# One core, a state-space block and a recurrent/attention block: the passage between them, where x1 is turned and made h

## The chip, the cores and the metric

The kernel runs on one core of a Trainium2 chip (trn2). The metric is the device time of one launch in microseconds. All inputs and outputs are float32.

## The reference, cut to what matters

Two blocks follow each other on x, 512 positions of 2048 columns. Both are computed in full; here is what stands around the passage between them.

```python
def first_block(x, ln_g, final_g, ...):
    x = x + ssm_mixer(rmsnorm(x, ln_g[0]), ...)     # ends with y @ ssm_w_out
    return rmsnorm(x, final_g)

def second_block(x, c, positions, w_ada, b_ada, w_in, ...):
    mod = silu(c) @ w_ada[l] + b_ada[l]
    shift, scale, gate = jnp.split(mod, 3, axis=-1)
    h = rms_norm(x) * (1.0 + scale[:, None, :]) + shift[:, None, :]
    proj = h @ w_in[l]                              # 2048 x 4160, float32
    ...                                             # recurrent branch, attention branch
    x = x + gate[:, None, :] * (y @ w_out[l])
```

## The kernel before, in words

**Matmuls.** Each float32 operand of a large product is split in two rounded parts, hi and lo, and a product is three matmuls of 128 x 128 x 512 into one bank of the accumulator memory (hi by hi, hi by lo, lo by hi). `three` (L2401) issues them; `three_hi_first` (L2406) issues the two that need only the hi part of the moving operand, then waits for its lo part and issues the third. It is used where the moving operand is only just being made.

**Weights** come in units. A unit of the second block's input projection holds 4 blocks of 128 rows by 256 columns, so two column blocks n = 0 and 1 of 128. Four units (16 blocks of rows) make a panel. Units go through a ring of 4 places: SP starts the load into `w_raw` (L669), ScalarE writes `w_hi` (L1090), VectorE writes `w_lo` (L1771). TensorE signals `unit_used` after a unit's last matmul.

**The passage.** The first block's projection out ends with its last panel. VectorE adds the residual, ScalarE sums squares, and meanwhile TensorE runs 36 turns of the identity (`keep_running(36)`, L2586). Then VectorE has the factor `x1rr` of each position (L1898), and x1, which lies with positions on the partitions, must become h with model columns on the partitions. A block of h is 128 model columns by 512 positions; there are 16 of them, kb = 0 to 15. The steps of one block:

- scaling: `xh <- x1t * x1rr`, in pieces of 512 columns (four blocks) by 128 positions. For the first 512 columns VectorE does positions t = 0 and 1 (`scale_x1`, L1902 to L1910) and ScalarE t = 2 and 3 (L1198). For the other columns VectorE does all four, partly between its other work (L1911 to L1921);
- turn: TensorE transposes the block, four 128 x 128 pieces (`turn_x1`, L2588, the transposes at L2596), into one of banks 4 to 7. The signal is `h_turned`;
- ScalarE writes `h_mod`, with the shift and scale (`modulate`, L1202 to L1207), and `h_hi` (`make_h_hi`, L1209 to L1211);
- VectorE writes `h_lo = h_mod - h_hi` (L1923).

ScalarE's order is written out by hand (L1213 to L1222): modulate(0), make_h_hi(0), modulate(1), and then for kb = 1 to 15 modulate(kb+1) and make_h_hi(kb), with the split of unit 2's weights behind kb = 3 and that of unit 3's behind kb = 7. VectorE's loop (L1913 to L1926) does for each kb the scaling that falls due and then `h_lo`; behind kb = 4 and 8 it makes `w_lo` of units 2 and 3. Units 0 and 1 have been split before. Each of these loops runs in order on its engine, and each instruction waits on semaphores that count blocks.

**TensorE's order** in the first panel (L2620 to L2623): blocks 0 to 3 are turned, then units 0 to 3 follow (`first_panel`, L2600). In a unit, column block n = 0 goes first: three matmuls with each of its 4 blocks of h, and behind each block of h the turn of the block four further on. Then n = 1 follows with 12 matmuls on blocks of h that are there already. Results of n = 0 gather in bank 0, those of n = 1 in bank 1. After the panel ScalarE copies the two banks to `xr` (L1232), and the other panels run on with all of h in place (`panels`, L2626).

Of the kernel before, what the change touches and what calls it, by code (L numbers as in the profile page):

```python
# [17 lines left out]
ACT = mybir.ActivationFunctionType  # L18
AX_X = mybir.AxisListType.X

P = 128
SEQ = 512
NT = SEQ // P
D = 2048
KB = D // P
# [18 lines left out]
UKT = 4  # L44
UCOL = 256
UNIT = UKT * UCOL
UPP = KB // UKT
# [29 lines left out]
TKT, TCOL = 2, 512  # L77
# [4 lines left out]
OUT_PANELS = D // TCOL  # L82
# [3 lines left out]
U_RNN = U_OUT1 + OUT_PANELS * OUT1_UPP  # L86
# [31 lines left out]
ADA_PARTS = P // ADA_ROWS  # L118
ADA_FETCH_AT, ADA_FOLD_AT = (1, 9), (5, 13)
ADA_COL = (0, 48, 128, 176, 256)  # L120
LAST_X1 = (OUT_PANELS - 1) * TCOL


# [68 lines left out]
def build_program(nc, x, ln_g, final_g, ssm_w_in, ssm_conv_w, ssm_conv_b, ssm_dt_bias, ssm_a_log, ssm_d,  # L192
# [4 lines left out]
    with ctx:  # L197
        sem_names = {}

        def sem(name):  # L200
            assert name not in sem_names
            sem_names[name] = ctx.enter_context(nc.semaphore(name))
            return sem_names[name]

        def sb(name, shape, dt=F32, scope=ctx):
            return scope.enter_context(nc.sbuf_tensor(name, shape, dt))
# [8 lines left out]
        ps = ctx.enter_context(nc.psum_tensor("ps", [P, 8, 512], F32))  # L215
# [3 lines left out]
        w_hi = sb("w_hi", [P, RING, UNIT], F32R)  # L219
        w_lo = sb("w_lo", [P, RING, UNIT], F32R)  # L220
# [9 lines left out]
        x1gs, x1rr = small[:, 56:60], small[:, 60:64]  # L230
# [88 lines left out]
        def ada_cols(k):  # L319

            return cols[:, ADA_COL[k]:ADA_COL[k] + ADA_FOLD]

# [14 lines left out]
        h_hi = sb("h_hi", [P, KB, SEQ], F32R, scope_f)  # L337
        h_lo = sb("h_lo", [P, KB, SEQ], F32R, scope_f)
# [57 lines left out]
        x1t = sb("x1t", [P, NT, D], F32, scope_e)  # L396
        xh = sb("xh", [P, NT, D], F32, scope_e)
# [32 lines left out]
        lo_ready = sem("lo_ready")  # L430
        unit_used = sem("unit_used")
# [70 lines left out]
        xh_ready = sem("xh_ready")  # L502
        h_turned = sem("h_turned")
        h_mod_ready = sem("h_mod_ready")
        h_hi_ready = sem("h_hi_ready")
        h_lo_ready = sem("h_lo_ready")
# [3 lines left out]
        f_bank_freed = sem("f_bank_freed")  # L510
# [59 lines left out]
        def unit_ap(ring, slot, cols_=UCOL):  # L570
            return ring[:, slot, 0:UKT * cols_].rearrange("p (k n) -> p k n", k=UKT)
# [351 lines left out]
        def _(act):  # L923
# [32 lines left out]
            for kb in range(KB):  # L956
                if kb % UKT == 0:
                    hi(0, kb // UKT)
                if kb == 3 * UKT:
# [5 lines left out]
                                     scale=cols[:, ROW_LN + kb:ROW_LN + kb + 1]).then_inc(hn_hi_ready, 1)  # L965
# [172 lines left out]
            def x1_last_squares():  # L1138

                i = OUT_PANELS - 1  # L1140
                for t in range(NT):
                    act.wait_ge(x1_added, i * NT + t + 1)
                    act.wait_ge(x1_squared, i * NT + t)
                    if t == 0:
# [4 lines left out]
                    act.wait_ge(x1g_squared, i * NT + t)  # L1149
                    nc.scalar.activation(ps[:, 5, :], xh[:, t, LAST_X1:], ACT.Square, accum_out=x1_part[:, 1, t:t + 1]  # L1150
                                         ).then_inc(x1g_squared, 1)
                act.dma_start(x1_tok[:, :, LAST_X1:], xh[:, :, LAST_X1:]).then_inc(x1_free, 16)

# [24 lines left out]
            for i in range(1, OUT_PANELS):  # L1178
                last = i == OUT_PANELS - 1
# [15 lines left out]
                nc.scalar.activation(r, r, ACT.Sqrt).then_inc(root_done, 1)  # L1195
            act.wait_ge(x1_rms_ready, 1)
            for t in (2, 3):
                nc.scalar.activation(xh[:, t, 0:TCOL], x1t[:, t, 0:TCOL], ACT.Copy, scale=x1rr[:, t:t + 1]  # L1198
                                     ).then_inc(xh_half_ready, 1)
            act.wait_ge(ada_cols_ready, 1)  # L1200

# [14 lines left out]
            for kb in range(1, KB):  # L1216
# [3 lines left out]
                if kb in (3, 7):  # L1220
                    u = (kb + 1) // UKT + 1
                    split_hi(U_RNN + u, u, landed_before(U_RNN) + 1)  # L1222
            act.wait_ge(h_turned, KB)
            act.wait_ge(xh_ready, NT * OUT_PANELS - 2)
            for u in range(UPP):
                if u == UPP - 1:
                    for n in range(2):
# [235 lines left out]
        def _(dve):  # L1463
# [345 lines left out]
            def x1_panel(i):  # L1809
                dve.wait_ge(x_in_landed, i * 16 + 16)  # L1810
                for t in range(NT):
# [8 lines left out]
                    if i == OUT_PANELS - 1:  # L1820
                        if t == 0:
                            dve.wait_ge(unit_used, U_RNN - OUT1_UPP // 2)
                        nc.vector.tensor_tensor(xh[:, t, LAST_X1:], x1p[:, t, :], gateb[:, LAST_X1:], ALU.mult
                                                ).then_inc(x1g_ready, 1)
# [74 lines left out]
            dve.sem_inc(f_bank_freed, 2)  # L1899
            dve.wait_ge(x1_rms_ready, 1)  # L1900

            def scale_x1(c, t):  # L1902
                at = slice(c * TCOL, (c + 1) * TCOL)
                if c == OUT_PANELS - 1 and t == 0:
                    dve.wait_ge(x1_free, 16 * (OUT_PANELS + 1))
                src = x1t[:, t, at] if c < OUT_PANELS - 1 else xh[:, t, at]
                nc.vector.tensor_scalar(xh[:, t, at], src, x1rr[:, t:t + 1], None, ALU.mult).then_inc(xh_ready, 1)

            for t in range(2):
                scale_x1(0, t)  # L1910
            for t in range(2):  # L1911
                scale_x1(1, t)
            for kb in range(KB):  # L1913
                if kb == 4:
                    dve.wait_ge(root_done, NT + 3)
                    st.done(nc.vector.reciprocal(x1rs, x1rs))
                if kb == 1:
                    for t in range(2, NT):
                        scale_x1(1, t)
                if 1 <= kb <= KB - 8:  # L1920
                    scale_x1((kb - 1) // 4 + 2, (kb - 1) % 4)  # L1921
                dve.wait_ge(h_hi_ready, kb + 1)
                nc.vector.tensor_tensor(h_lo[:, kb, :], h_mod[:, kb % 4, :], h_hi[:, kb, :].bitcast(F32),  # L1923
                                        ALU.subtract).then_inc(h_lo_ready, 1)
                if kb in (UKT, 2 * UKT):
                    split_lo(U_RNN + kb // UKT + 1, kb // UKT + 1)  # L1926
# [430 lines left out]
        def _(pe):  # L2357
# [43 lines left out]
            def three(out_, a_hi, a_lo, b_hi, b_lo, start, stop):  # L2401
                nc.tensor.matmul(out_, a_hi, b_hi, start=start, stop=False)  # L2402
                nc.tensor.matmul(out_, a_hi, b_lo, start=False, stop=False)  # L2403
                return nc.tensor.matmul(out_, a_lo, b_hi, start=False, stop=stop)  # L2404

            def three_hi_first(out_, w_hi_, w_lo_, a_hi, a_lo, start, stop, hi_sem, lo_sem, count):  # L2406

                pe.wait_ge(hi_sem, count)
                nc.tensor.matmul(out_, w_hi_, a_hi, start=start, stop=False)  # L2409
                nc.tensor.matmul(out_, w_lo_, a_hi, start=False, stop=False)  # L2410
                pe.wait_ge(lo_sem, count)
                return nc.tensor.matmul(out_, w_hi_, a_lo, start=False, stop=stop)  # L2412
# [156 lines left out]
            for u in range(len(LAST_SCAN), OUT1_UPP):  # L2569
                if u == Y_HALF // TKT + 3:  # L2570

                    pe.wait_ge(y_squared, 2)
                    for t in range(NT):
                        mm = nc.tensor.matmul(ps[:, 4, t:t + 1], ysq[:, t * P:(t + 1) * P], ones[:, 0:1],
                                              start=True, stop=True)
# [11 lines left out]

            def turn_x1(kb):  # L2588

                pe.wait_ge(xh_ready, kb // 4 * NT + 2)  # L2590
                if kb == 0:
                    pe.wait_ge(xh_half_ready, 2)
                if kb >= 4:
                    pe.wait_ge(h_lo_ready, kb - 3)
                for t in range(NT):
                    mm = nc.tensor.transpose(ps[:, 4 + kb % 4, t * P:(t + 1) * P], xh[:, t, kb * P:(kb + 1) * P],  # L2596
                                             ident[:])
                mm.then_inc(h_turned, 1)

            def first_panel(u):  # L2600

                pe.wait_ge(lo_ready, U_RNN + u + 1)
                for n in range(2):
                    if u == 0:
                        pe.wait_ge(f_bank_freed, n + 1)
                    for k in range(UKT):
                        kb = u * UKT + k
                        w = [unit_ap(r, u)[:, k, n * P:(n + 1) * P] for r in (w_hi, w_lo)]
                        if n == 0:
                            mm = three_hi_first(ps[:, n, :], *w, h_hi[:, kb, :], h_lo[:, kb, :],  # L2610
                                                kb == 0, kb == KB - 1, h_hi_ready, h_lo_ready, kb + 1)
                        else:
                            mm = three(ps[:, n, :], *w, h_hi[:, kb, :], h_lo[:, kb, :], kb == 0, kb == KB - 1)
                        if n == 0 and kb + UKT < KB:
                            turn_x1(kb + UKT)
                    if n == 0 and u == UPP - 1:
                        mm.then_inc(f_bank_done, 1)
                mm.then_inc(unit_used, 1)

            for kb in range(UKT):  # L2620
                turn_x1(kb)
            for u in range(UPP):
                first_panel(u)  # L2623
            pe.wait_ge(h_lo_ready, KB)

# [29 lines left out]
            for u in range(KR_UNITS):  # L2655
                pe.wait_ge(lo_ready, U_KR + u + 1)
                for k in range(UKT):
                    kb = u * UKT + k
                    w = unit_ap(w_hi, u, 2 * ROPE)[:, k, :]
                    if kb == 0:  # L2660
                        nc.tensor.matmul(ps[:, 2, :], w, h_hi[:, kb, :], start=True, stop=False)
                    mm = nc.tensor.matmul(ps[0:ROPE, 2, :], w[:, 0:ROPE], h_lo[:, kb, :], start=False, stop=False)
                    if kb:
                        mm = nc.tensor.matmul(ps[:, 2, :], w, h_hi[:, kb, :], start=False, stop=kb == KB - 1)
# [262 lines left out]
```

## Time and profile before

| | |
|---|---|
| median of 3 runs | 2118.04 us (2118.0 to 2118.15) |
| the profiled execution's own time | 2117.97 us |
| its span, first to last instruction | 2116.4 us |
| TensorE matmul busy | 2103.2 us, 99% of the span |
| VectorE busy | 1302.8 us, 62% |
| ScalarE busy | 806.0 us, 38% |
| DMA | 139 GB/s over the span |

Engines are named PE (TensorE matmul), PEld (its weight loads, which overlap the matmuls), DVE (VectorE), ACT (ScalarE), POOL (GpSimd) and SP. Times in the trace are microseconds from the span's start. A matmul of 512 columns is shown with 0.40 us, but the next starts 0.233 us later: their ends overlap, so the step from start to start is what one costs. The same holds for the vector engines, whose next instruction often starts before the last is shown ended. L12 is line 12 of the kernel; transposes of the passage are "MATMUL ps<-ident,xh" at L2596, those of `three_hi_first` are at L2409, L2410 and L2412.

### The profile page before, as it was taken

The numbers are of one execution on the slowest core, as the hardware profiler recorded it, in microseconds if no ns is written. First come the engines' busy times: TensorE is split into PE (matmuls) and PEld (weight loads), VectorE is DVE, ScalarE is ACT, GpSimd is POOL, SyncE is SP. The second block draws the span as 40 slices with busy tenths as digits, with TensorE's granted clock in tenths as the row PEclk, the third lists the DMA queues.
The fourth block names the chain that finished last, engine by engine and source line by source line (L and its number), as shares of the span: only waits on it lengthen the run. The fifth ranks groups of instructions, "written<-read, shape, count | busy, mean of one in ns | idle before, by whom it ended". The sixth has DMA issues, their size and how long they took to land.

```text
span 2116.4 us, 27861 instructions
## 1 busy us (share of the span) xinstructions
PE 2103.2 (99%) x10059; PEld 1683.0 (80%) x10059; DVE 1302.8 (62%) x2147; ACT 806.0 (38%) x1089; POOL 88.0 (4%) x130
## 2 busy tenths in 40 slices
PE   8999999999999999999999999999999999999999
PEld 7888888888888888888878888878887778876887
DVE  5567867777786777778874323253227788667333
ACT  5233433333343342434443222262224556665121
POOL 0000000000000000000000000000000001110000
PEclk9999999999999999999999999999999999999999
DMA  7555645555564555555564354343333232112332
GB/s 221 166 156 152 184 149 167 162 168 163 159 175 147 171 158 165 162 170 170 187 218 155 111 162 133 107 144 108 99 89 84 78 104 79 63 60 74 126 119 99
DMA packets 234242, 294.50 MB, mean 139 GB/s; under 512 B 36883, under 2 KB 170883, under 8 KB 233411
## 3 DMA queue, kind: packets, MB, share of 16 engines
q1 hardware_dynamic: 200402, 252.98, 38.6%
q0 software_dynamic: 8624, 29.04, 4.9%
q10 hardware_dynamic: 25152, 11.64, 2.1%
q8 instruction: 39, 0.64, 0.1%
q14 instruction: 25, 0.20, 0.0%
HBM read 273.54 MB, written 20.08 MB: 139 GB/s over the span
## 4 chain that ended last, share of the span: by engine, by line
PE 95%; DVE 3%; DMA 1%; ACT 1%; issue 0%; SPq 0%; DVEq 0%; ACTq 0%
PE ps L2402 29%; PE ps L2404 29%; PE ps L2403 29%; PE ps L2503 2%; PE ps L2485 1%; PE ps L2736 1%; PE ps L2761 1%; DMA xt<-in_x_dram 1%; PE ps L2740 1%; PE ps L2752 0%; PE ps L2648 0%; PE ps L2487 0%; PE ps L2412 0%; PE ps L2409 0%; PE ps L2410 0%
## 5 line engine op out<-in xcount | busy, mean ns | idle before, releaser
L2402 PE MATMUL ps<-hn_hi,w_hi 128*128 128x512 f32 x1264 | 500.9, 396 | 0.0
L2404 PE MATMUL ps<-hn_hi,w_lo 128*128 128x512 f32 x1264 | 499.3, 395 | 0.0
L2403 PE MATMUL ps<-hn_lo,w_hi 128*128 128x512 f32 x1264 | 499.2, 395 | 0.0
L1771 DVE TENSOR_TENSOR w_lo<-w_raw,w_hi 128x1024 fp32r<-128x1024 f32 x174 | 212.8, 1226 | 399.6 <-ACT w_hi L1090 398.3
L1090 ACT ACTIVATE w_hi<-w_raw 128x1024 fp32r<-128x1024 f32 x174 | 183.2, 1057 | 450.2 <-PE ps L2404 412.1
L953 ACT ACTIVATE w_hi<-w_raw 128x1024 fp32r<-128x1024 f32 x162 | 170.9, 1056 | 413.1 <-PE ps L2404 396.4
L1509 DVE TENSOR_TENSOR w_lo<-w_raw,w_hi 128x1024 fp32r<-128x1024 f32 x162 | 198.1, 1223 | 205.6 <-ACT w_hi L953 205.5
L2402 PEld LDWEIGHTS ps<-hn_hi,w_hi 128*128 128x128 f32 x1264 | 237.0, 187 | 58.4 <-issue 1.2
L2404 PEld LDWEIGHTS ps<-hn_hi,w_lo 128*128 128x128 f32 x1264 | 236.9, 187 | 57.9
L2403 PEld LDWEIGHTS ps<-hn_lo,w_hi 128*128 128x128 f32 x1264 | 237.0, 187 | 57.2
L2402 PE MATMUL ps<-w_hi,y_hi 128*128 128x512 f32 x512 | 203.0, 396 | 0.4 <-DVE y_lo L1780 0.4
L2404 PE MATMUL ps<-w_hi,y_lo 128*128 128x512 f32 x512 | 202.5, 395 | 0.0
L2403 PE MATMUL ps<-w_lo,y_hi 128*128 128x512 f32 x512 | 202.5, 395 | 0.0
L2402 PE MATMUL ps<-h_hi,w_hi 128*128 128x512 f32 x496 | 197.1, 397 | 0.0
L2403 PE MATMUL ps<-h_lo,w_hi 128*128 128x512 f32 x496 | 195.9, 395 | 0.0
L2404 PE MATMUL ps<-h_hi,w_lo 128*128 128x512 f32 x496 | 195.9, 395 | 0.0
L1606 DVE SCALAR_TENSOR_TENSOR ada_acc<-ada_raw,silu_c,ada_acc 128x768 f32<-128x768 f32 x120 | 121.4, 1012 | 0.3 <-DMA ada_raw<-in_w_ada_dram 0.3
L2402 PEld LDWEIGHTS ps<-h_hi,w_hi 128*128 128x128 f32 x496 | 93.0, 187 | 28.8 <-issue 6.5
L2402 PEld LDWEIGHTS ps<-w_hi,y_hi 128*128 128x128 f32 x512 | 96.2, 188 | 24.6 <-DVE y_lo L1780 1.3
L2404 PEld LDWEIGHTS ps<-w_hi,y_lo 128*128 128x128 f32 x512 | 96.2, 188 | 23.3
L2403 PEld LDWEIGHTS ps<-w_lo,y_hi 128*128 128x128 f32 x512 | 96.2, 188 | 22.9
L2404 PEld LDWEIGHTS ps<-h_hi,w_lo 128*128 128x128 f32 x496 | 93.0, 187 | 22.6
(392 smaller groups left out, 2765.0 us busy)
## 6 DMA issues: line engine op xcount, KB each, us to landing
ada_raw<-in_w_ada_dram SPq DMA_DIRECT2D x128, 384.0 KB, 3.4
w_raw<-in_ssm_w_in_dram SPq DMA_DIRECT2D x96, 512.0 KB, 4.6
w_raw<-in_ssm_w_in_dram SPq DMA_DIRECT2D x128, 256.0 KB, 4.0
w_raw<-in_w_in_dram SPq DMA_DIRECT2D x64, 512.0 KB, 3.8
w_raw<-in_ssm_w_out_dram SPq DMA_DIRECT2D x60, 512.0 KB, 3.5
csb<-cs_rows POOLq DMA_DIRECT2D x32, 512.0 KB, 7.2
w_raw<-in_w_out_dram SPq DMA_DIRECT2D x32, 512.0 KB, 4.0
y_rows<-yt POOLq DMA_DIRECT2D x8, 1024.0 KB, 4.7
```

Source lines behind the costliest of these rows:

```text
L953: nc.scalar.activation(w_hi[:, s, :], w_raw[:, s, :], ACT.Copy).then_inc(hi_ready, 1)
L1090: nc.scalar.activation(w_hi[:, slot, :], w_raw[:, slot, :], ACT.Copy).then_inc(hi_ready, 1)
L1509: nc.vector.tensor_tensor(w_lo[:, s, :], w_raw[:, s, :], w_hi[:, s, :].bitcast(F32), ALU.subtract).then_inc(lo_ready, 1)
L1606: ins = nc.vector.scalar_tensor_tensor(ada_acc[:], ada_raw[:, k % 2, :], silu_c[:, k:k + 1], ada_acc[:], ALU.mult, ALU.add)
L1771: nc.vector.tensor_tensor(w_lo[:, slot, :], w_raw[:, slot, :], w_hi[:, slot, :].bitcast(F32), ALU.subtract).then_inc(lo_ready, 1)
L2402: nc.tensor.matmul(out_, a_hi, b_hi, start=start, stop=False)
L2403: nc.tensor.matmul(out_, a_hi, b_lo, start=False, stop=False)
L2404: return nc.tensor.matmul(out_, a_lo, b_hi, start=False, stop=stop)
L2485: nc.tensor.transpose(ps[:, 4, b * P:(b + 1) * P], xst[:, b, at], ident[:])
L2503: mm = nc.tensor.matmul(ps[h * HD:(h + 1) * HD, 6, b * P:(b + 1) * P], lhs[:, 2 * b + h, :], rhs[:, 2 * b + h, :], start=first, stop=c == ...
L2736: nc.tensor.matmul(ps[:, bank, 0:n], qt[:, h, at], kt[:, h, 0:n], start=True, stop=False)
L2740: nc.tensor.matmul(ps[:, bank, 0:n], qpt[rows, at], kpt[rows, 0:n], start=False, stop=True).then_inc(scored, 1)
```

## The change

Three things, all in the passage. The first 128 columns are scaled alone: ScalarE scales only those for t = 2 and 3, VectorE those for t = 0 and 1 and then, in four instructions, the remaining 384 of the first 512 columns for all four t. Unit 0 is a function of its own, `first_unit`: each of its 4 blocks of h is multiplied with both column blocks (four matmuls on h_hi, two on h_lo), and the next turn follows. And only three blocks are turned ahead, in place of four, in all units of the panel. The counts of the waits follow.

```diff
@@ -118,6 +118,7 @@
+H_AHEAD = 3
@@ -1195,7 +1196,7 @@
             for t in (2, 3):
-                nc.scalar.activation(xh[:, t, 0:TCOL], x1t[:, t, 0:TCOL], ACT.Copy, scale=x1rr[:, t:t + 1]
+                nc.scalar.activation(xh[:, t, 0:P], x1t[:, t, 0:P], ACT.Copy, scale=x1rr[:, t:t + 1]
                                      ).then_inc(xh_half_ready, 1)
@@ -1221,7 +1222,7 @@
-            act.wait_ge(xh_ready, NT * OUT_PANELS - 2)
+            act.wait_ge(xh_ready, NT * OUT_PANELS + 2)
@@ -1899,15 +1900,17 @@
-            def scale_x1(c, t):
-                at = slice(c * TCOL, (c + 1) * TCOL)
+            def scale_x1(c, t, first=0, last=TCOL):
+                at = slice(c * TCOL + first, c * TCOL + last)
...
             for t in range(2):
-                scale_x1(0, t)
+                scale_x1(0, t, last=P)
+            for t in range(NT):
+                scale_x1(0, t, first=P)
             for t in range(2):
                 scale_x1(1, t)
@@ -2587,7 +2590,7 @@
             def turn_x1(kb):
 
-                pe.wait_ge(xh_ready, kb // 4 * NT + 2)
+                pe.wait_ge(xh_ready, kb // 4 * NT + NT + 2 if kb else 2)
                 if kb == 0:
                     pe.wait_ge(xh_half_ready, 2)
@@ -2601,8 +2604,6 @@
                 for n in range(2):
-                    if u == 0:
-                        pe.wait_ge(f_bank_freed, n + 1)
                     for k in range(UKT):
...
-                        if n == 0 and kb + UKT < KB:
-                            turn_x1(kb + UKT)
+                        if n == 0 and kb + H_AHEAD < KB:
+                            turn_x1(kb + H_AHEAD)
...
-            for kb in range(UKT):
+            def first_unit():
+
+                pe.wait_ge(lo_ready, U_RNN + 1)
+                pe.wait_ge(f_bank_freed, 2)
+                for kb in range(UKT):
+                    w = [[unit_ap(r, 0)[:, kb, n * P:(n + 1) * P] for r in (w_hi, w_lo)] for n in range(2)]
+                    pe.wait_ge(h_hi_ready, kb + 1)
+                    for n in range(2):
+                        nc.tensor.matmul(ps[:, n, :], w[n][0], h_hi[:, kb, :], start=kb == 0, stop=False)
+                        nc.tensor.matmul(ps[:, n, :], w[n][1], h_hi[:, kb, :], start=False, stop=False)
+                    pe.wait_ge(h_lo_ready, kb + 1)
+                    for n in range(2):
+                        mm = nc.tensor.matmul(ps[:, n, :], w[n][0], h_lo[:, kb, :], start=False, stop=False)
+                    if kb == UKT - 1:
+                        mm.then_inc(unit_used, 1)
+                    turn_x1(kb + H_AHEAD)
+
+            for kb in range(H_AHEAD):
                 turn_x1(kb)
-            for u in range(UPP):
+            first_unit()
+            for u in range(1, UPP):
                 first_panel(u)
             pe.wait_ge(h_lo_ready, KB)
```

## Rows read from the trace of the kernel before

**Rows 1.** The page, busy time, share of the span and instructions of each engine.

```profile
PE 2103.2 (99%) x10059; PEld 1683.0 (80%) x10059; DVE 1302.8 (62%) x2147; ACT 806.0 (38%) x1089; POOL 88.0 (4%) x130
```

**Rows 2.** Waits of PE, whole run: total us, times, longest.

```profile
PE ps L2596 <- ACT xh L1198: 1.2, 1, 1.2
```

**Rows 3.** Timeline of PE, 1391 to 1408: start, us, instruction, [idle before <-releaser].

```profile
1391.16 4.09 PE L2581 MATMUL ps<-ident 128*128 128x128 f32 x36
...
1396.45 1.94 PE L2596 MATMUL ps<-ident,xh 128*128 128x128 f32 x16 [1.20 <-ACT xh L1198]
...
1398.76 0.47 PE L2409 MATMUL ps<-h_hi,w_hi 128*128 128x512 f32 x1 [0.37 <-ACT h_hi L1211]
...
1399.39 0.50 PE L2412 MATMUL ps<-h_lo,w_hi 128*128 128x512 f32 x1
...
1401.25 0.19 PEld L2412 LDWEIGHTS ps<-h_lo,w_hi 128*128 128x128 f32 x1 [0.37 <-DVE h_lo L1923]
1401.25 0.50 PE L2412 MATMUL ps<-h_lo,w_hi 128*128 128x512 f32 x1
...
1401.59 0.60 PE L2596 MATMUL ps<-ident,xh 128*128 128x128 f32 x4
...
1407.19 0.39 PE L2409 MATMUL ps<-h_hi,w_hi 128*128 128x512 f32 x1
```

**Rows 4.** Timeline of PE, unit 2, a turn, a block and the next turn.

```profile
1415.21 0.60 PE L2596 MATMUL ps<-ident,xh 128*128 128x128 f32 x4
1415.56 0.47 PE L2409 MATMUL ps<-h_hi,w_hi 128*128 128x512 f32 x1
1415.88 0.39 PE L2410 MATMUL ps<-h_hi,w_lo 128*128 128x512 f32 x1
...
1416.34 0.60 PE L2596 MATMUL ps<-ident,xh 128*128 128x128 f32 x4
```

**Rows 5.** Timeline of ACT, 1394 to 1439.

```profile
1394.97 1.33 ACT L1198 ACTIVATE xh<-x1t,small 128x512 f32<-128x512 f32 x2 [0.15 <-DVE small L1898]
1397.17 0.78 ACT L1206 ACTIVATE h_mod<-ps,small 128x512 f32<-128x512 f32 x1 [0.87 <-PE ps L2596]
1397.98 0.63 ACT L1211 ACTIVATE h_hi<-h_mod 128x512 fp32r<-128x512 f32 x1
...
1401.55 0.78 ACT L1206 ACTIVATE h_mod<-ps,small 128x512 f32<-128x512 f32 x1
1402.21 0.64 ACT L1211 ACTIVATE h_hi<-h_mod 128x512 fp32r<-128x512 f32 x1
1402.73 1.06 ACT L1090 ACTIVATE w_hi<-w_raw 128x1024 fp32r<-128x1024 f32 x1
1403.68 0.78 ACT L1206 ACTIVATE h_mod<-ps,small 128x512 f32<-128x512 f32 x1
...
1415.85 0.78 ACT L1206 ACTIVATE h_mod<-ps,small 128x512 f32<-128x512 f32 x1 [1.51 <-PE ps L2596]
...
1437.98 0.51 ACT L1240 ACTIVATE rope_t<-ysq 128x128 f32<-128x128 f32 x2 [5.22 <-DVE ysq L1982]
```

**Rows 6.** Timeline of DVE, 1394 to 1436.

```profile
1394.97 1.68 DVE L1907 TENSOR_SCALAR xh<-x1t,small 128x512 f32<-128x512 f32 x4
1398.65 0.69 DVE L1923 TENSOR_TENSOR h_lo<-h_mod,h_hi 128x512 fp32r<-128x512 f32 x1 [2.00 <-ACT h_hi L1211]
...
1405.01 0.69 DVE L1923 TENSOR_TENSOR h_lo<-h_mod,h_hi 128x512 fp32r<-128x512 f32 x1 [0.98 <-ACT h_hi L1211]
1405.62 1.22 DVE L1771 TENSOR_TENSOR w_lo<-w_raw,w_hi 128x1024 fp32r<-128x1024 f32 x1
1406.76 0.48 DVE L1907 TENSOR_SCALAR xh<-xh,small 128x512 f32<-128x512 f32 x1
...
1435.23 0.23 DVE L1968 TENSOR_SCALAR ysq<-ysq 128x128 f32<-128x128 f32 x1
```

**Rows 7.** Windows: us, busy us (instructions) of each engine, PEclk, DMA share, GB/s.

```profile
1391.00:1399.00 8.00, 6.43 (x55) 5.92 (x54) 4.94 (x14) 6.29 (x16) 0.00 (x0) 1.00 0.58 155
```

## The prediction

> **What bounds the kernel now.** I read the page's busy times first: TensorE is busy 99% of the span [rows 1]. Only a pause of TensorE, or instructions taken from it, can move the end. TensorE's waits over the whole run come next: the middle, where x1 becomes h, holds one of the longer ones, 1.2 us for the scaled x1 [rows 2]. Then the middle's timeline. From 1391.16, where the first projection out has ended, to 1407.19, where unit 1 of the second block begins, 16.03 us pass [rows 3]. The work in them: 24 matmuls of 512 columns, whose step without a stall is 0.233 us, and 68 turns (36 of them on the identity alone). A dense block of three matmuls and four turns takes 1.13 us, so four turns are 0.43 us [rows 4]. That is 5.6 + 7.3 = 12.9 us of work, so 3.1 us of pause. That is the whole prize; after 1407.19 units 1 to 3 ran without a pause (4 x 1.13 + 12 x 0.233 = 7.32 us for a unit with turns).
>
> **How a block of h is made** (block 0 to 15). TensorE turns it (T), ScalarE writes h_mod, then h_hi, VectorE writes h_lo. The steps: T to h_mod 0.64 us [rows 4, 5]; an h_mod occupies ScalarE 0.67, an h_hi 0.52, a w_hi 0.95; h_hi's start to its first matmul 0.78 (0.75 in the schedule below; the difference is 0.1 in the sum), to h_lo 0.67; h_lo's start to its matmul 0.74 [rows 3, 5, 6]. ScalarE's order decides: h_mod(b+1) stands ahead of h_hi(b), so h_hi(b) cannot start before block b+1 is turned. In the kernel before that never showed on TensorE after unit 0: with four blocks turned ahead it is ScalarE that waits, 1.51 us at block 12 [rows 5].
>
> **The change, part by part.** It removes no matmul and no turn. It reorders.
>
> First 128 columns alone. ScalarE's two scalings take 1.33 us from 1394.97; T0 starts at 1396.45 [rows 3, 5]. For 128 columns I take the two 128x128 activations of the rope tables, 0.51 us together [rows 5]: T0 at 1394.97 + 0.51 + 0.12 = 1395.60. The bounds: nothing at all, or no cheaper than now, 1.33. VectorE's scalings go from two of 512 (0.40 a step, 0.48 long) to two of 128 (0.23 long, from a 128x128 operation) and four of 384 (0.40 long, between the two) [rows 6]: the last is done at 1394.97 + 0.30 + 0.96 + 0.40 = 1396.63, T1 starts at 1396.68, T2 ends its issue near 1397.44. That costs nothing, because block 0's matmuls wait for h_hi(0): h_mod(0) 1396.28, h_hi(0) 1397.09, matmul 1397.84, against 1398.76 before. The cover is 0.40 us; if all four cost as much as 512 columns, 0.32 of it is used. VectorE's further scalings end before h_lo(0) is due.
>
> First unit with both column blocks. A block is now six matmuls and one T: 0.32 + 5 x 0.233 + 0.35 = 1.83 us, which is longer than the 1.19 us in which ScalarE makes a block (0.67 + 0.52). So the pauses between blocks go. T3 starts 1399.35, T4 1401.21, T5 1403.04, T6 1404.87, and unit 0 ends at 1405.22. Unstalled alternation between two banks is not in the trace; the nearest rows, matmuls that follow each other in one bank, give 0.233, and I take that. Gain: 1407.19 - 1405.22 = 1.97 us, less 0.43 for a turn (block 7) still owed: **1.5 us**, half of the prize.
>
> Three blocks ahead. T(b+3) now stands behind block b, and h_hi(b+2) needs it. From block b's first matmul: 0.70 to T(b+3), 0.64 to h_mod(b+3), 0.67 to h_hi(b+2), 0.75 to block b+2's first matmul, 2.76 us. In units 1 to 3 two blocks with turns last only 2.2 to 2.3. So this **loop of waits stalls TensorE 0.5 to 0.6 us** wherever it is entered with no reserve. With four ahead the loop spans three blocks, 3.40 us, and fits. In the six-matmul blocks it fits too (3.65).
>
> A stall also exposes the weight load: after the wait at 1401.25 the next instruction comes 0.34 us later, not 0.233 [rows 3]. A rule of the Trainium skill ("TensorE: Matmul & The Clock Gate", what happens when you issue a matmul) says that TensorE pulls weight loads ahead of running matmuls; here the load of L2412 starts with its matmul at 1401.25, behind the wait [rows 3]. By the rule the five stalls on h_lo below would cost 0.5 us less and the sum would be 2.3; I go by the row.
>
> - Unit 1. ScalarE, from T4: h_mod(4) 1401.85, h_hi(3) 1402.52, w_hi of unit 2 1403.04, h_mod(5) 1403.99, h_hi(4) 1404.66, so block 4 starts at 1405.41, 0.19 late, and its h_lo is 0.09 late. T6 at 1404.87 gives h_mod(6) 1405.51, h_hi(5) 1406.18, block 5 1406.93 (0.17 late). VectorE has put w_lo of unit 2 (1.14) and a scaling (0.40) between h_lo(4) at 1405.33 and h_lo(5) at 1407.48 [rows 6]: the matmul on it starts at 1408.22, 0.71 late. That order is in the kernel before also, where block 5 came late enough to cover it. T8 at 1408.56, h_mod(8) 1409.20, h_hi(7) 1409.87, block 7 1410.62: 0.58 late. Unit 1 ends at 1414.85 and took 9.63 us for 7.32: **+2.3**.
> - Unit 2. The second half of unit 1 refills two blocks of h, so blocks 8 and 9 are on time. Block 10 needs T11, issued behind block 8: 0.58 late, its h_lo 0.09, the exposed load 0.11: **+0.8**, end 1422.97.
> - Unit 3. T15 stands behind block 12, block 13 has no turn, so block 14 is due 1.83 us after block 12 and comes after 2.76: 0.93 late, with h_lo and load about **+1.2**, the owed turn being done here. End 1430.23, where before it is 1407.19 + 2 x 7.32 + 5.60 = 1427.43.
>
> Sum: -1.5 + 2.3 + 0.8 + 1.2 = **+2.8 us**. Behind it: w_hi of unit 4 starts 1426.0, w_lo ends near 1428.4, the bank copy near 1429.5, all ahead of 1430.2, so nothing is added. The kernel is TensorE-bound to the end [rows 1], so the lag passes on. On SP and the GpSimd queue nothing is moved; loads of raw weights wait for w_lo and follow it.
>
> The profiled execution took 2117.97 us for a span of 2116.4; 0.07 below the median of 2118.04. 2117.97 + 2.8 + 0.07 = **2120.8 us**. With ScalarE's 128 columns at their bounds the sum is 2.4 to 3.6 (T0 at 1395.1, where T1 then waits for VectorE as before, or 1396.4); with the loop 0.2 us shorter or longer at each of its four passes (blocks 5, 7, 10, 14) it moves by 0.8 either way. Own range: 2120.0 to 2122.0. A measurement of this kernel tells 0.2%, 4.2 us, from no change, so this counts as no change, and the prize of 3.1 us cannot reach that bound either.
>
> **Rivals.**
> 1. The loop is covered: the reserve built in unit 0 lasts. Then the 1.5 us stay, 2116.5. For it: ScalarE is idle 1.51 us before block 12 now [rows 5], so it looks fast enough. Against: that idle time is a wait for a turn, and the change issues turns later. Chance 0.11.
> 2. The loop binds in half of its places (units 2 and 3, whose stalls need the turn order alone, but not VectorE's order in unit 1, or the reverse): about zero, 2117.5 to 2119. Chance 0.11.
> 3. **Slower by over 0.2%**: the granted clock falls. It is 1.00 in the middle's window [rows 7], although TensorE ran nothing but turns and pauses from 1391.16 to 1398.76. The new pauses in units 1 to 3 (up to 0.9 us) come where there was none. At 1.2 GHz instead of 2.4 each matmul step of 0.233 can grow by 0.233, so it decides from about six matmuls on, on top of 2.8 (1.4 / 0.233); 30 of them give 2128. Chance 0.03. The same page of the Trainium skill (its part on PE-mode transposes) says that transposes don't count as busy for the clock. By that rule the turns from 1391.16 to 1398.76 would be one long pause; the granted clock over them is 1.00 all the same, so the trace does not bear it out, and the change shortens them by 0.9 us.
> 4. The turns ahead do what they say but six-matmul blocks still wait (the first part fails): ScalarE's 1.19 would have to be 1.83. Then 2122 to 2123, with 0.03.
>
> Forecast 0.72. The high tail of forecast and rival 4 above 2122.3 adds 0.04 to the slow side: slower 0.07, faster 0.01, same 0.92. Range: 2118.3 to 2122.4 leaves out rival 1, part of rival 2, and rival 3.
>
> **What the changed profile would show.** T0 near 1395.6 and the first h matmul near 1397.9 after an unchanged start; unit 0 with blocks of 1.83 us and no wait, ended about 1405.2. Then waits of TensorE for h_hi and h_lo in the groups of L2409 to L2412's helper in units 1, 2 and 3, some 0.5 to 0.9 us each, at blocks 5, 7, 10 and 14; ScalarE's h_mod waiting for TensorE's turns for more than the one long wait of now; unit 4 near 1430.2. Unit 1 dense from 1405.3, or unit 4 near 1426, would make it wrong; so would a clock under 1.00.

## The result, and the profile after

| | before | after |
|---|---|---|
| median, 22 runs each | 2117.96 us (2117.79 to 2118.32) | 2121.01 us (2120.89 to 2121.27) |
| ratio, 95% interval | | 1.0014 (1.0008 to 1.0020) |
| span of the profiled execution | 2116.4 us | 2119.7 us |

The change makes the kernel 3.05 us slower. The two sets of runs don't overlap, so the loss is plain to see, though it is 0.14% and below the 0.2% that was taken as the bound between a change and none. The forecast was 2.8 us, 2120.8.

TensorE's busy time on the page, to be held against [rows 1]:

```profile
PE 2105.7 (99%) x10059; PEld 1683.4 (79%) x10059; DVE 1303.8 (62%) x2151; ACT 805.7 (38%) x1089; POOL 88.1 (4%) x130
```

The instructions of TensorE are the same 10059. Its busy time grew by 2.4 us although no work came in. Two things hide part of a pause in it. A matmul that starts behind a wait is drawn longer, 0.50 in place of 0.40. And the end that is drawn for an instruction lies behind the point at which the next could have started: the four turns at 1417.00 are drawn to 1417.60, the next matmul could have come at 1417.35 and came at 1417.85, so a pause of 0.50 us is shown as 0.25. The starts of instructions are the thing to read.

TensorE's waits in the middle (1390 to 1440) of the changed kernel: total us, times, longest.

```profile
PE ps L2412 <- ACT h_hi L1212: 1.2, 3, 0.7
PE ps L2599 <- DVE xh L1908: 0.9, 2, 0.5
PE ps L2415 <- DVE h_lo L1926: 0.6, 1, 0.6
PE ps L2629 <- ACT h_hi L1212: 0.2, 1, 0.2
```

In the kernel before, the wait for the scaled x1 stood first, 1.2 us [rows 2]. Now the waits for h_hi and h_lo in units 1 to 3 (lines 2412 and 2415) are together the larger part: 1.8 us as shown, 4.35 by the starts in the table below (4.78 of loss in units 1 to 3, less 0.43 for the turn that moved there). Where they are, the timeline of TensorE shows. The origin has moved by 0.14 us (1391.30 for 1391.16), which is taken off in the comparisons below.

```profile
1391.30 4.09 PE L2584 MATMUL ps<-ident 128*128 128x128 f32 x36
1395.93 0.63 PE L2599 MATMUL ps<-ident,xh 128*128 128x128 f32 x4 [0.54 <-DVE xh L1908]
1396.95 1.09 PE L2599 MATMUL ps<-ident,xh 128*128 128x128 f32 x8 [0.39 <-DVE xh L1908]
1398.25 0.47 PE L2629 MATMUL ps<-h_hi,w_hi 128*128 128x512 f32 x1 [0.20 <-ACT h_hi L1212]
...
1401.56 0.60 PE L2599 MATMUL ps<-ident,xh 128*128 128x128 f32 x4
...
1403.38 0.60 PE L2599 MATMUL ps<-ident,xh 128*128 128x128 f32 x4
...
1405.21 0.60 PE L2599 MATMUL ps<-ident,xh 128*128 128x128 f32 x4
1405.77 0.47 PE L2412 MATMUL ps<-h_hi,w_hi 128*128 128x512 f32 x1
...
1406.40 0.50 PE L2415 MATMUL ps<-h_lo,w_hi 128*128 128x512 f32 x1
1406.74 0.60 PE L2599 MATMUL ps<-ident,xh 128*128 128x128 f32 x4
1407.19 0.50 PE L2412 MATMUL ps<-h_hi,w_hi 128*128 128x512 f32 x1
...
1408.53 0.51 PE L2415 MATMUL ps<-h_lo,w_hi 128*128 128x512 f32 x1 [0.61 <-DVE h_lo L1926]
...
1410.01 0.60 PE L2599 MATMUL ps<-ident,xh 128*128 128x128 f32 x4
1410.87 0.50 PE L2412 MATMUL ps<-h_hi,w_hi 128*128 128x512 f32 x1 [0.26 <-ACT h_hi L1212]
...
1415.17 0.39 PE L2412 MATMUL ps<-h_hi,w_hi 128*128 128x512 f32 x1
...
1417.00 0.60 PE L2599 MATMUL ps<-ident,xh 128*128 128x128 f32 x4
1417.85 0.50 PE L2412 MATMUL ps<-h_hi,w_hi 128*128 128x512 f32 x1 [0.25 <-ACT h_hi L1212]
...
1423.34 0.39 PE L2412 MATMUL ps<-h_hi,w_hi 128*128 128x512 f32 x1
...
1426.02 0.50 PE L2412 MATMUL ps<-h_hi,w_hi 128*128 128x512 f32 x1 [0.69 <-ACT h_hi L1212]
...
1430.58 0.39 PE L2405 MATMUL ps<-h_hi,w_hi 128*128 128x512 f32 x1
```

Unit 0 has turns 1.83 us apart with no wait between blocks; its last turn starts at 1405.21 and leaves TensorE at 1405.56. Unit 1 ends at 1415.17, unit 2 at 1423.34, unit 3 at 1430.58.

| stretch | before | after | difference |
|---|---|---|---|
| 36 turns to the end of unit 0 | 16.03 | 14.26 | -1.77 |
| unit 1 | 7.32 | 9.61 | +2.29 |
| unit 2 | 7.32 | 8.17 | +0.85 |
| unit 3 (one owed turn, 0.43, in it) | 5.60 | 7.24 | +1.64 |
| sum | 36.27 | 39.28 | **+3.01** |

So practically the whole loss is made in this passage. The table compares the two profiled executions, whose spans differ by 3.3 us (the changed one, 2121.27 us, was the slowest of its 22). 3.01 of the 3.3 lie here, 0.14 ahead of the passage and the rest behind it, which is within the 0.4 us by which executions of one kernel differ; between the medians it is 3.05. ScalarE's timeline shows the loop itself:

```profile
1409.52 0.78 ACT L1207 ACTIVATE h_mod<-ps,small 128x512 f32<-128x512 f32 x1 [0.84 <-PE ps L2599]
1410.19 0.62 ACT L1212 ACTIVATE h_hi<-h_mod 128x512 fp32r<-128x512 f32 x1
...
1416.50 0.78 ACT L1207 ACTIVATE h_mod<-ps,small 128x512 f32<-128x512 f32 x1 [2.37 <-PE ps L2599]
1417.18 0.62 ACT L1212 ACTIVATE h_hi<-h_mod 128x512 fp32r<-128x512 f32 x1
...
1424.67 0.78 ACT L1207 ACTIVATE h_mod<-ps,small 128x512 f32<-128x512 f32 x1 [2.63 <-PE ps L2599]
1425.35 1.14 ACT L1212 ACTIVATE h_hi<-h_mod 128x512 fp32r<-128x512 f32 x2
```

At 1416.50 ScalarE had stood for 2.37 us, waiting for the turn of block 11, with h_mod(10) long done. Behind h_mod(11) stands h_hi(10), 1417.18, and TensorE gets block 10 at 1417.85, 0.5 us late. At 1424.67 the same with the turn of block 15 and h_hi(14), and block 14 is 0.86 us late. Two engines stand idle in turn, each waiting for the other. The sum of ScalarE's waits for turns in the passage, before (1395 to 1430) and after (1394 to 1436):

```profile
ACT h_mod L1206 <- PE ps L2596: 3.6, 3, 1.5
ACT h_mod L1207 <- PE ps L2599: 8.7, 9, 2.6
```

### The profile page after: what moved, and what is told of

Same layout as the page of the kernel before. It is cut to its first block, busy times and chain, and to the rows that moved or that the text cites. A ratio compares the mean times of both kernels' runs of the same rounds, so it can differ in the third digit from the quotient of the medians.

```text
span 2119.7 us, 27865 instructions
## 1 busy us (share of the span) xinstructions
PE 2105.7 (99%) x10059; PEld 1683.4 (79%) x10059; DVE 1303.8 (62%) x2151; ACT 805.7 (38%) x1089; POOL 88.1 (4%) x130
## 4 chain that ended last, share of the span: by engine, by line
PE 95%; DVE 3%; ACT 1%; DMA 1%; issue 0%; SPq 0%; DVEq 0%; ACTq 0%
PE ps L2405 29%; PE ps L2407 29%; PE ps L2406 29%; PE ps L2506 2%; PE ps L2488 1%; PE ps L2755 1%; PE ps L2780 1%; DMA xt<-in_x_dram 1%; PE ps L2759 1%; PE ps L2771 0%; PE ps L2667 0%; PE ps L2490 0%; PE ps L2415 0%; DVE w_lo L1772 0%; DVE y_lo L1781 0%
```

## The experiments

Each kernel was timed beside the kernel before on the same chip. The medians of before were 2117.93 to 2117.97 there. The intervals of the ratios are some 0.001 to each side, which is wider than these differences; the runs of one kernel lie within 0.4 us of their median (except with two blocks ahead), and it is the runs and the traces together that decide. Differences from the kernel before of 0.5 us and more are those of runs that don't overlap; where two sets of runs overlap, it is said.

Two theories. **Loop**: the turn of block b+3 stands behind block b, ScalarE does h_mod(b+1) ahead of h_hi(b), so the path from block b over the turn, h_mod and h_hi to block b+2 takes longer than TensorE's two blocks. **Pace**: ScalarE needs 1.19 us for a block, TensorE 1.13, so whoever makes TensorE early in unit 0 sees it wait in unit 1 whatever is turned when.

### Four blocks ahead in the changed kernel

```diff
-H_AHEAD = 3
+H_AHEAD = 4
```

> The changed kernel with four blocks turned ahead in place of three, nothing else. Loop theory (the turn of block b+3 stands behind block b, and h_hi(b+2) waits for it): the stalls at blocks 7, 10 and 14 are gone, what is left is unit 0's gain, 1.2 to 1.6 us below the kernel before (about 2116.6). Pace theory (the rival: ScalarE makes a block of h in 1.19 us, TensorE takes one in 1.13, so a TensorE that is early waits for ScalarE in any case): still 2 to 3 us above the kernel before.

Measured: 2116.53 us, ratio 0.9993 (0.9984 to 1.0002), 1.4 us below the kernel before and 4.5 below the changed one. TensorE's waits from 1390 to 1432 are shown as this one line:

```profile
PE ps L2599 <- DVE xh L1908: 0.9, 2, 0.5
```

ScalarE's waits for turns, 1394 to 1432, have shrunk from nine to three:

```profile
ACT h_mod L1207 <- PE ps L2599: 2.8, 3, 1.7
```

The pace theory falls: TensorE is early here as well and doesn't give it back. One small stall is left that no wait shows: the turns around block 5 start 1.36 us apart (1406.25 and 1407.61) in place of 1.13, where h_lo(5) stands behind w_lo on VectorE.

Not all of the 4.5 us is waiting. With four ahead the fourth turn (0.43 us) runs in the pause before block 0: block 0 starts 6.95 us after the start of the 36 turns in both kernels. With three ahead that turn is done later, at full price, in unit 3. So 0.43 is a turn taken out of a pause and 4.1 the stalls.

### Three blocks ahead in the kernel before

```diff
-                        if n == 0 and kb + UKT < KB:
-                            turn_x1(kb + UKT)
+                        if n == 0 and kb + 3 < KB:
+                            turn_x1(kb + 3)
...
-            for kb in range(UKT):
+            for kb in range(3):
                 turn_x1(kb)
```

> The kernel before with three blocks turned ahead, nothing else. Loop theory: the loop binds in unit 0 too, where a block has three matmuls; about 3.9 us above the kernel before (2121.9), with TensorE's waits for h_hi in all four units. Pace theory: within 0.5 us of the kernel before, since TensorE is not early.

Measured: 2121.99 us, ratio 1.0019 (1.0010 to 1.0028), 4.0 us above. TensorE's waits, 1390 to 1432:

```profile
PE ps L2409 <- ACT h_hi L1211: 2.4, 6, 0.8
PE ps L2596 <- ACT xh L1198: 1.2, 1, 1.2
```

The six waits for h_hi are in all four units, at blocks 0, 1, 3, 7, 10 and 14. Three ahead costs 4.0 us in the old kernel and 4.5 in the new one. It is this part alone that loses, and it loses without the other two.

### The 128 columns alone, and the new unit 0 alone

Each of these two parts of the change was put into the kernel before, four ahead in both. The edits are those of the diff above.

> The kernel before with the first 128 columns scaled alone, nothing else (four ahead, old unit 0). Loop theory: the first turn starts 0.5 us earlier, and since ScalarE's chain of h_mod and h_hi starts with it, 0.4 to 0.8 us below the kernel before (about 2117.3). Pace theory: the same 0.5, or nothing if the wait for the other 384 columns takes it back.

Measured: 2117.42 us, ratio 0.9998 (0.9989 to 1.0007), 0.5 us below.

> The kernel before with the new unit 0 (both column blocks on each block of h), nothing else (four ahead, scaling by 512 columns). Loop theory: the pauses between blocks of unit 0 go, 0.6 to 1.0 us below the kernel before (about 2117.2). Pace theory: TensorE is then early in unit 1 and gives it all back: within 0.2 us of the kernel before, or above.

Measured: 2117.19 us, ratio 0.9996 (0.9987 to 1.0005), 0.8 us below. Together they are worth 1.4 us (four ahead, above), the two alone 0.5 + 0.8 = 1.3. They hardly interact.

### Three ahead, h_hi directly behind its h_mod

```diff
-            modulate(1)
             for kb in range(1, KB):
-                if kb + 1 < KB:
-                    modulate(kb + 1)
+                modulate(kb)
                 make_h_hi(kb)
```

> The changed kernel, still three ahead, but ScalarE does h_mod(kb) and h_hi(kb) of the same block together, so h_hi(b) no longer stands behind h_mod(b+1). Loop theory: the loop then spans three blocks, most stalls go, about 0.4 us below the kernel before (2117.6), with one wait of 0.3 to 0.5 us left near block 15. Pace theory: ScalarE's block costs 0.14 more, so the time rises above the changed kernel's 2121.0.

Measured: 2117.58 us, ratio 0.9998 (0.9989 to 1.0007), 3.4 us below the changed kernel and 0.4 below the kernel before. (Its slowest run, 2117.80, reaches the fastest of the kernel before, 2117.76.) This cuts the loop at its other side: three blocks are turned ahead as before, but h_hi(b) no longer stands behind h_mod(b+1). TensorE's trace shows no wait for h in units 1 to 3; by the starts block 15 is 0.30 us late (1423.08, with 1422.55 before it), the one that was expected. To be slower than the kernel before takes both, three ahead and that order. Three ahead without that order still costs 1.05 us against four ahead (2116.53), 0.43 of it the turn.

### w_lo of units 2 and 3 later on VectorE

```diff
-                if kb in (UKT, 2 * UKT):
-                    split_lo(U_RNN + kb // UKT + 1, kb // UKT + 1)
+                if kb in (2 * UKT - 1, 3 * UKT - 1):
+                    split_lo(U_RNN + (kb + 1) // UKT, (kb + 1) // UKT)
```

> The changed kernel with w_lo of units 2 and 3 made by VectorE behind h_lo(7) and h_lo(11) in place of h_lo(4) and h_lo(8). Takes away the 0.6 us wait for h_lo(5) alone. Loop theory: 0.6 us below the changed kernel (about 2120.4), the waits at blocks 7, 10 and 14 stay. If VectorE's order were the main cause, the kernel would be near the kernel before, 2118.

Measured: 2120.42 us, ratio 1.0011 (1.0002 to 1.0020), 0.6 us below the changed kernel. The wait of 0.61 us for h_lo(5) is gone and the waits at blocks 10 and 14 are there as before:

```profile
1417.07 0.50 PE L2412 MATMUL ps<-h_hi,w_hi 128*128 128x512 f32 x1 [0.25 <-ACT h_hi L1212]
1425.24 0.50 PE L2412 MATMUL ps<-h_hi,w_hi 128*128 128x512 f32 x1 [0.68 <-ACT h_hi L1212]
```

The wait at block 7, which was expected to stay, is no longer shown as one. The loop still binds there: blocks 4 to 7 start at 1405.60, 1407.03, 1408.56 and 1410.08, some 1.5 us apart where 1.13 would do, and unit 1 takes 9.00 us, for 9.61 in the changed kernel and 7.32 before. VectorE's order makes 0.6 us of the changed kernel's time. With four ahead the same edit gives 0.2 (below), so 0.4 of the 4.5 us that three ahead costs go by that order.

### The dose: two blocks ahead

```diff
-H_AHEAD = 3
+H_AHEAD = 2
```

> The changed kernel with two blocks turned ahead: a dose of the suspected cost. The loop then spans one block, so every block takes about 2.8 to 3.6 us from turn to turn. Loop theory: 20 to 23 us above the kernel before (about 2139.7), a stall of 1.7 us at nearly every block. Pace theory: less than 2 us above the changed kernel.

Measured: 2146.23 us, ratio 1.0138 (1.0123 to 1.0154), 28.3 above the kernel before: the loop theory's direction, and 6.5 us more than its number. The windows of this kernel show why (us, busy us of PE, PEld, DVE, ACT, POOL, granted clock, DMA share, GB/s):

```profile
1400.00:1405.00 5.00, 2.23 (x12) 1.60 (x11) 1.16 (x3) 2.59 (x4) 0.00 (x0) 1.00 0.86 312
...
1415.00:1420.00 5.00, 3.61 (x10) 2.54 (x11) 2.13 (x4) 1.29 (x2) 0.00 (x0) 0.50 0.36 103
...
1425.00:1430.00 5.00, 5.00 (x18) 3.91 (x17) 1.83 (x2) 1.29 (x2) 0.00 (x0) 0.68 0.06 10
1430.00:1435.00 5.00, 2.27 (x12) 1.28 (x10) 0.69 (x1) 2.59 (x4) 0.00 (x0) 1.00 0.30 95
1435.00:1440.00 5.00, 3.58 (x10) 2.50 (x11) 1.39 (x2) 1.29 (x2) 0.00 (x0) 0.50 0.01 3
...
1445.00:1450.00 5.00, 2.29 (x12) 1.28 (x10) 0.69 (x1) 2.58 (x5) 0.00 (x0) 1.00 0.00 0
```

The granted clock, the number behind POOL's count, fell to 0.50, which is 1.2 GHz. Up to there TensorE had waited 1.4 us in front of each of blocks 1 to 5. It rose while unit 1's second half ran without a wait, and fell again in unit 2. In unit 3 TensorE waited 1.39 us in front of two blocks and the clock stayed at 1.00. At 0.50 a step is 0.43 us, and a block takes 3.89 us (from 1414.98 to 1418.87) where one at 1.00 takes 3.06 (from 1431.98 to 1435.04). In the timeline of the same kernel:

```profile
1414.98 0.80 PE L2412 MATMUL ps<-h_hi,w_hi 128*128 128x512 f32 x1 [1.39 <-ACT h_hi L1212]
...
1418.87 0.79 PE L2412 MATMUL ps<-h_hi,w_hi 128*128 128x512 f32 x1 [1.39 <-ACT h_hi L1212]
1419.46 0.63 PE L2413 MATMUL ps<-h_hi,w_lo 128*128 128x512 f32 x1
1419.88 0.63 PE L2415 MATMUL ps<-h_lo,w_hi 128*128 128x512 f32 x1
1420.31 1.05 PE L2599 MATMUL ps<-ident,xh 128*128 128x128 f32 x4
...
1431.98 0.50 PE L2412 MATMUL ps<-h_hi,w_hi 128*128 128x512 f32 x1 [1.39 <-ACT h_hi L1212]
...
1435.04 0.80 PE L2412 MATMUL ps<-h_hi,w_hi 128*128 128x512 f32 x1 [1.39 <-ACT h_hi L1212]
```

### Two blocks ahead with the waits filled

The kernel of the last section, and behind each turn in front of a wait:

```diff
+            def fill(turns):
+
+                for _ in range(turns):
+                    nc.tensor.transpose(ps[:, 3, 0:P], ident[:], ident[:])
...
                             turn_x1(kb + H_AHEAD)
+                            if k < UKT - 1:
+                                fill(12)
...
                     turn_x1(kb + H_AHEAD)
+                    fill(12)
```

> Two blocks turned ahead again, with 12 turns of the identity (about 1.3 us) behind each turn where TensorE waits 1.4 us for h_hi, into a bank that nothing else uses. Clock theory: the 6.5 us that two ahead cost beyond the loop came from the granted clock, which stood at 0.50 in part of units 1 and 2; with the waits filled it stays at 1.00 and the time is what the loop alone gives, 2139 to 2140. If the 6.5 us were longer waits of the loop itself, the time stays near 2146, and the fill adds to it where it does not fit.

Measured: 2139.72 us, ratio 1.0103 (1.0087 to 1.0120). Windows, same columns:

```profile
1415.00:1420.00 5.00, 4.85 (x30) 3.37 (x29) 2.18 (x4) 1.72 (x3) 0.00 (x0) 1.00 0.37 105
...
1435.00:1440.00 5.00, 5.00 (x26) 3.81 (x25) 1.04 (x2) 1.30 (x2) 0.00 (x0) 1.00 0.00 0
```

With more instructions the kernel is 6.5 us faster, and the time lies where the loop alone was expected to put it (20 to 23 us above the kernel before; that it meets the 2139.7 to 0.1 us is luck). The granted clock is 1.00 in all windows of the passage, the two shown among them. So the extra was the clock. Its size is less sure than its cause: the kernel with empty waits ran four times, from 2145.19 to 2149.34 us, the filled one four times, from 2139.28 to 2140.6, on another chip (the kernel before gave 2117.97 and 2117.93 there), and the two profiled spans, 2143.7 and 2138.3, differ by 5.4 us.

### Four ahead with VectorE's order, and with ScalarE's

Two combinations: four ahead with w_lo later, and the same with h_hi directly behind its h_mod. The edits are those shown above.

> The changed kernel with four blocks turned ahead and w_lo of units 2 and 3 later (behind h_lo(7) and h_lo(11)). Loop theory: 1.6 us below the kernel before (about 2116.4), 0.2 below four ahead alone: the best of these. Pace theory: above the kernel before.

Measured: 2116.32 us, ratio 0.9992 (0.9983 to 1.0001), 1.65 us below the kernel before and 0.2 below four ahead alone. The runs of these two overlap (2116.27 to 2116.49, and 2116.36 to 2116.70), but the trace shows where the 0.2 lies: the turns around block 5, 1.36 us apart with four ahead alone, are 1.13 apart here (1406.16 and 1407.29).

> Four ahead, w_lo of units 2 and 3 later, and ScalarE's h_hi of a block directly behind its h_mod. Loop theory: with four ahead no wait for h is left that this order could shorten, so within 0.15 us of four ahead with w_lo later (2116.3). Pace theory: ScalarE's 0.14 us more for each block shows, 1 to 2 us more.

Measured: 2116.30 us, ratio 0.9992 (0.9983 to 1.0002). No difference from the one above. These two are the best versions found, about 1.6 us faster than the kernel before; TensorE's only wait left in the passage in the first of them is the 0.9 us for the scaled x1.

## Why the prediction was right

It was right in sign, size and place: 2.8 us forecast, 3.05 measured. Step by step, with starts relative to the end of the first projection out:

- **First 128 columns.** ScalarE's two scalings were taken at 0.51 us from the rope tables' activations; they took 0.69 (0.39 long, 0.30 apart), and T0 came 0.14 behind them. (The profile puts T0's wait down to VectorE, but VectorE's two pieces were done at 1395.58, ScalarE's at 1395.79, and in the kernel before T0 also came 0.15 behind ScalarE's end.) It started 0.83 us after x1's factor was there, 0.63 was forecast. VectorE's pieces took 0.28 (128 columns) and 0.42 (384), against 0.23 and 0.40. Both lie within the bounds. This is the one mis-sized term: block 0's first matmul came 3.15 us after the factor, forecast 2.87, before 3.79. Alone the part is worth 0.5 us.
- **Unit 0 without pauses.** Blocks of 1.83 us as forecast, no wait between them, bank alternation costs nothing: turns at 1401.56, 1403.38, 1405.21. The gain up to the end of unit 0 was 1.77 us in place of 1.97. The first term's 0.28 makes this 0.2; the rest came back, since unit 0 itself took 7.31 us from its first matmul and 7.38 was forecast.
- **The loop.** Late blocks, forecast and measured: block 4 0.19 and 0.21; block 5 0.17 and 0.10, its h_lo 0.71 and 0.77; block 7 0.58 and 0.51; block 10 0.58 and 0.50; block 14 0.93 and 0.86. The units come out closer than their blocks do, since the misses, each under 0.1 us, go both ways. Unit 1 took 9.61 us (9.63 forecast), unit 2 8.17 (8.12), unit 3 7.24 (7.26). Undoing three ahead alone took all of it away, doing it alone brought it into the old kernel, and cutting it on ScalarE took 3.4 us away. The cause is shown, not argued. The forecast speaks of "the one long wait of now" on ScalarE; the kernel before has three (0.87, 1.17 and 1.51 us). No term of the sum uses it.
- **The w_lo in VectorE's way**, forecast 0.71, measured 0.77 in the trace. VectorE's row of the changed kernel shows the order, and moving it gave 0.6 us:

```profile
1405.66 0.69 DVE L1926 TENSOR_TENSOR h_lo<-h_mod,h_hi 128x512 fp32r<-128x512 f32 x1 [0.98 <-ACT h_hi L1212]
1406.27 1.22 DVE L1772 TENSOR_TENSOR w_lo<-w_raw,w_hi 128x1024 fp32r<-128x1024 f32 x1
1407.40 0.48 DVE L1908 TENSOR_SCALAR xh<-xh,small 128x512 f32<-128x512 f32 x1
1407.80 0.68 DVE L1926 TENSOR_TENSOR h_lo<-h_mod,h_hi 128x512 fp32r<-128x512 f32 x1
```

- **The exposed weight load.** The row was trusted over the Trainium skill's rule (page "TensorE: Matmul & The Clock Gate", what happens when you issue a matmul) that loads are pulled ahead. Where no wait stands in between, the changed kernel's trace agrees with the rule: the load at 1407.30 is that of the matmul at 1407.53. Across a wait it bears the row out: at each of the five stalls on h_lo the next instruction started 0.33 to 0.35 us later, and the weight load of the waiting matmul at 1408.53 started with it, not ahead:

```profile
1407.30 0.19 PEld L2413 LDWEIGHTS ps<-h_hi,w_lo 128*128 128x128 f32 x1
1408.53 0.19 PEld L2415 LDWEIGHTS ps<-h_lo,w_hi 128*128 128x128 f32 x1 [1.04 <-DVE h_lo L1926]
```

- **The lag passes on.** +3.01 us in the passage and +3.3 at the end of the profiled pair, +3.05 between the medians; nothing of it is made up later.

Of the rivals none came. Unit 0's reserve did not cover the loop, nor did half of it stay away. The granted clock stayed at 1.00 in the changed kernel. That rival was priced with the right mechanism all the same (a step of 0.233 us grows to 0.43): at two ahead, where the waits are longer and stand in front of every block, it made about 6 us. The expectation for that run forgot it, though the prediction had named it.

## What to carry to other kernels

How far ahead a producer must run is set by a path, not by an average: follow one item from the instruction that starts it to the one that uses it, over every in-order queue and with what stands ahead of it there, and compare with the consumer's time for as many items as lie between. ScalarE was idle for microseconds at a time and still late, since its queue held the needed h_hi behind an h_mod whose block TensorE had not yet turned. When a change consists of three parts, each can be timed alone on the old kernel; here two of them gain 1.4 us and the third loses 4.5. And work that is moved out of a pause costs its full time where it goes: the fourth turn was free before block 0 and cost 0.43 us in unit 3.

## What the runs showed of the hardware that was not expected

- With waits of 1.4 us before blocks 1 to 5 in a row, each by itself short, TensorE lost its full clock: granted 1.00 over unit 0 and the start of unit 1, then 0.50 (1.2 GHz) from block 5 on, with steps of 0.43 us for 0.233; again in unit 2; not in unit 3, with the same waits before two blocks. With the changed kernel's pauses of 0.5 to 0.9 us at blocks 5, 7, 10 and 14 it stayed at 1.00.
- Turns of the identity in those waits kept the clock at 1.00 and saved 6.5 us between the medians. The Trainium skill ("TensorE: Matmul & The Clock Gate", the part on PE-mode transposes) says that transposes don't count as busy for the clock. This run does not agree with it.
- TensorE's busy time went up by 2.4 us with the same 10059 instructions: behind a wait a matmul is drawn with 0.50 us for 0.40, and the drawn end of the instruction ahead covers up to 0.25 us of a pause. So a busy time near 100% does not exclude a growing pause.
- Two ScalarE activations of the same 128 x 128 elements can differ by a third: 0.39 us for the scaling, 0.30 for the rope tables' activations. They differ in their function and in that the scaling reads a factor for each position. No run separates the two.
